# A hybrid decoder layer with product-key retrieval: the order ahead of the first slots, four weight products on GpSimd, and the last tile ended in pieces of three groups and one

## The reference, cut to what matters

```python
c_act = silu(c)
shift1, scale1, gate1, shift2, scale2, gate2 = split(c_act @ w_ada + b_ada)
h = modulate(rms_norm(x, g_norm1), shift1, scale1)
a, u, v = split(h @ w_in)                       # 1024 tokens, 512 columns each
mixed = concat(pool_mixer(a), spatial_gating(u, v))
x = x + gate1 * (mixed @ w_out)
h = modulate(rms_norm(x, g_norm2), shift2, scale2)
# product-key retrieval, for each token and each of 8 heads:
q = h @ w_query                                 # two halves ("sides") a head
s = q_side @ sub_keys_side                      # 128 scores a side
cand = top16(s_0) + top16(s_1)                  # 256 sums, the best 16 give idx
gate = softmax(best16)
act = gelu(expert_down[idx] . h)                # 16 rows of 1024
x = x + gate2 * sum(gate * act * expert_up[idx])
out = rms_norm(x, g_final)
```

## Time and profile before

| | |
|---|---|
| median of 3 runs | 2828.95 us (2825.89 to 2829.47) |
| the profiled execution | 2833.91 us, span 2832.1 us |
| busy in the span | PE 68%, DVE 67%, ACT 43%, POOL 40% |
| DMA | 1162.38 MB, mean 410 GB/s |
| HBM read, written | 1151.97 MB, 7.86 MB |

### The profile page before, as it was taken

One profiled execution on the slowest core, in us unless ns is written; L12 is line 12 of the kernel. 1 busy time (PEld: TensorE's weight loads), 2 busy tenths in 40 slices (PEclk: granted clock), 3 DMA queues, 4 the chain that ended last, 5 costly groups with the idle time before them and its releaser, 6 DMA issues.

```text
span 2832.1 us, 38640 instructions
## 1 busy us (share of the span) xinstructions
PE 1938.6 (68%) x13316; PEld 893.8 (32%) x13316; DVE 1894.8 (67%) x4714; ACT 1210.7 (43%) x3867; POOL 1123.1 (40%) x1030
## 2 busy tenths in 40 slices
PE   5898898888886566666656666665666666665553
PEld 4555354444442222232323222221322323221110
DVE  5686776785766567677666757677676756676454
ACT  1245445454453344454444434444343544344333
POOL 0044334344443254444444444444444444344342
PEclk9998898899886566665666667665766666576555
DMA  9899999999999999999999999999999999999997
GB/s 404 339 373 403 396 413 417 409 420 420 420 401 397 416 422 421 421 421 421 421 421 421 421 421 419 416 421 421 417 415 421 419 421 416 421 415 421 421 420 294
DMA packets 169221, 1162.38 MB, mean 410 GB/s; under 512 B 19009, under 2 KB 25665, under 8 KB 35778
## 3 DMA queue, kind: packets, MB, share of 16 engines
q0 software_dynamic: 147456, 1073.81, 91.9%
q1 hardware_dynamic: 21570, 86.11, 7.7%
HBM read 1151.97 MB, written 7.86 MB: 410 GB/s over the span
## 4 chain that ended last, share of the span: by engine, by line
DMA 54%; PE 22%; DVE 11%; ACT 6%; issue 3%; SPq 3%; POOL 0%; another core or an unknown queue 0%; DVEq 0%; POOLq 0%; ACTq 0%
DMA work<-experts,expert_rows 41%; DMA more_ring<-experts,expert_rows 8%; PE ps_sum L900 7%; DVE work L1560 5%; PE ps_small L866 5%; PE ps_m L815 4%; DMA work<-w_ada 2%; PE ps_m L759 2%; DMA weights<-experts,expert_rows 1%; ACT diag L1137 1%; ACT weight L1132 1%; DMA vn_u<-x_scratch 1%; PE ps_wide L841 1%; SPq L613 1%; PE ps_m L770 1%
## 5 line engine op out<-in xcount | busy, mean ns | idle before, releaser
L650 POOL DMA_INDIRECT work<-experts,expert_rows x818 | 899.0, 1099 | 1378.7 <-PE ps_sum L900 1225.8
L1560 DVE CUSTOM_DVE_ANT_0 work<-work 128x1024 f32<-128x1024 f32 x818 | 997.5, 1221 | 589.3 <-DMA work<-experts,expert_rows 573.4
L900 PE MATMUL ps_sum<-work,diag 128*32 128x256 f32 x6544 | 717.5, 523 | 674.7 <-ACT diag L1137 653.6
L1130 ACT ACTIVATE act_out<-act_in 128x1 f32<-128x1 f32 x1024 | 207.4, 203 | 1162.8 <-DVE act_in L1560 1141.9
L900 PEld LDWEIGHTS ps_sum<-work,diag 128*32 128x32 f32 x6544 | 150.1, 126 | 1146.5 <-ACT diag L1137 1052.1
L1137 ACT ACTIVATE diag<-const,weight 128x32 f32<-128x32 f32 x1024 | 329.2, 321 | 33.5
L1132 ACT ACTIVATE weight<-gate,act_out 128x1 f32<-128x1 f32 x1024 | 301.6, 295 | 33.3
L866 PE MATMUL ps_small<-h_t,weights 128*128 128x128 f32 x1344 | 291.2, 384 | 0.0
L866 PEld LDWEIGHTS ps_small<-h_t,weights 128*128 128x128 f32 x1344 | 249.3, 278 | 125.7 <-issue 120.4
L1560 DVE CUSTOM_DVE_ANT_0 more_ring<-more_ring,work 128x1024 f32<-128x1024 f32 x122 | 149.1, 1222 | 91.5 <-DMA more_ring<-experts,expert_rows 90.4
L650 POOL DMA_INDIRECT more_ring<-experts,expert_rows x122 | 134.8, 1105 | 180.3 <-PE ps_sum L900 175.5
(11 more groups left out here) (200 smaller groups left out, 1991.1 us busy)
## 6 DMA issues: line engine op xcount, KB each, us to landing
work<-w_ada SPq DMA_DIRECT2D x12, 2048.0 KB, 23.6
work<-sides SPq DMA_DIRECT2D x26, 576.0 KB, 8.4
work<-experts,expert_rows POOLq DMA_INDIRECT x818
weights<-sides SPq DMA_DIRECT2D x16, 576.0 KB
more_sides<-sides SPq DMA_DIRECT2D x12, 576.0 KB
weights<-w_in SPq DMA_DIRECT2D x3, 2048.0 KB, 17.2
x_buf<-x SPq DMA_DIRECT2D x8, 512.0 KB, 11.4
weights<-w_out SPq DMA_DIRECT2D x2, 2048.0 KB, 37.5
```

What stands on the lines that cost most here:

```text
L650: nc.gpsimd.indirect_dma_start(ring[x.ring], None, experts, bass.IndirectOffsetOnAxis(ap=rows_flat[:, x.column:x.column + 1], axis=0),).th ...
L900: last = nc.tensor.matmul(ps_sum[quarter(c), x.group, :], diag[:, x.ring, :], ring[x.ring][:, D + c * QCOLS:D + (c + 1) * QCOLS], start=x. ...
L1130: nc.scalar.activation(act_out[:, s:s + 1], act_in[:, s:s + 1], ACT.Gelu).then_inc(s_gelu, 1)
L1560: nc.vector.tensor_tensor_reduce(down, down, h2_spread[x.segment % 2], 1.0, 0.0, ALU.mult, ALU.add, act_in[:, x.g % TURN:x.g % TURN + 1]). ...
```

## The change

It has these parts:

- **The prologue's order.** On PE, side (1, 0) goes between the two halves of the first spread, side (1, 1) ahead of the move of routing 1, and that move ahead of scores (1, 1). Side (1, 3) goes into the slots (`SIDE_AT[0]`), and three of tile 1's four PROJECT_V steps too (`MIX_HEAD` is 6 in place of 9). ScalarE follows this order; `exp_logits(1)` comes right behind the second half of the first spread. SP issues one side load fewer ahead of the loop.
- **Slot numbers.** The mixers of tiles 2, 3 and 4 begin two slots later, tile 1's three later. Turn 1's route steps begin at slot 5 in place of 2. By the rule above the move of routing 2 then lies at slot 29.
- **The products of w_out and gate1.** GpSimd makes the four of them, behind the output projection of tile 0 and ahead of its first gather. VectorE's four are gone.
- **The last tile.** Its first piece has groups 0 to 2 and starts at slot 1008, its last piece group 3, which sums in a bank of its own (`ps_last`). The last piece's four stores are issued two by SP and two by ScalarE.

```diff
-MIX_HEAD = PROJECT_A
-MIX_AT = {1: -MIX_HEAD, 2: 31, 3: 70, 4: 109, 5: 150, 6: 190, 7: 230}
-SCALE_W_SLOTS = (3, 6, 9, 12)
+MIX_HEAD = PROJECT_V + 1
+MIX_AT = {1: -MIX_HEAD, 2: 33, 3: 72, 4: 111, 5: 150, 6: 190, 7: 230}
+SCALE_W_PARTS = 4
...
-SPLIT_SLOT = SLOTS * TILES - PAIR * PAIR * GATHERS
+SPLIT_SLOT = SLOTS * TILES - PAIR * GATHERS
-ENDS = [(t, 0, QUADS) for t in range(TILES - 1)] + [(TILES - 1, 0, 2), (TILES - 1, 2, QUADS)]
+ENDS = [(t, 0, QUADS) for t in range(TILES - 1)] + [(TILES - 1, 0, QUADS - 1), (TILES - 1, QUADS - 1, QUADS)]
...
-ROUTE_AT = [None, 2, 28, 50, 74, 98]
+ROUTE_AT = [None, 5, 28, 50, 74, 98]
...
+LAST_GROUP = {x.g for x in TABLE if (x.tile, x.group) == (TILES - 1, QUADS - 1)}
+SIDE_AT[0] = (1, 3)
...
+        ps_last = ps_m3[:, 0:QCOLS]
...
+        def store_last(queue, quarters):
+            t, first, last = ENDS[TILES]
+            queue.wait_ge(s_final, TILES + 1)
+            for c in quarters:
+                queue.dma_start(out_v[t, c][:, first:last, :], y[quarter(c), first:last, :]).then_inc(s_out, 16)
...
             # SP
-            for n in range(2, 6 + SIDE_BUFS):
+            for n in range(2, 5 + SIDE_BUFS):
                 load_side(*FIRST_USE[n])
...
-            store_out(TILES)
+            store_last(sp, range(QUADS // 2))
...
             # GpSimd
+            pool.wait_ge(s_o, 1)
+            pool.wait_ge(s_mod, 2)
+            for n in range(SCALE_W_PARTS):
+                part = w_out_sb[:, 2 * n:2 * n + 2, :]
+                nc.gpsimd.tensor_tensor(part, part, gate1[:, :].unsqueeze(1).to_broadcast([P, 2, D]),
+                                        ALU.mult).then_inc(s_scaled_w, 1)
             pool.wait_ge(s_gate2_ps, 2)
...
             # PE
-            for half in range(2):
-                spread_first_h2(0, half)
+            spread_first_h2(0, 0)
+            side(1, 0)
+            spread_first_h2(0, 1)
             mixer(TURN_H, 1)
-            for b in range(2):
-                side(1, b)
-                scores(1, b)
+            scores(1, 0)
+            side(1, 1)
+            move_choices(1)
+            scores(1, 1)
             for n in range(TURN_H + 1, MIX_HEAD):
                 mixer(n, 1)
-                if n == PROJECT_V + 1:
-                    move_choices(1)
-            for b in range(2, 4):
-                side(1, b)
-                scores(1, b)
+            side(1, 2)
+            scores(1, 2)
...
             # ScalarE
-            for half in range(2):
-                copy_spread(0, half)
-            for n in range(SCALE_H + 1, MIX_HEAD):
-                mixer(n, 1)
-            for b in range(4):
-                if b == 2:
-                    exp_logits(1)
-                copy_query(1, b)
-                copy_score(1, b)
+            copy_spread(0, 0)
+            copy_query(1, 0)
+            copy_spread(0, 1)
+            exp_logits(1)
+            copy_score(1, 0)
+            mixer(COPY_H, 1)
+            copy_query(1, 1)
+            mixer(COPY_H + 1, 1)
+            copy_score(1, 1)
+            copy_query(1, 2)
+            copy_score(1, 2)
...
-            act.wait_ge(s_ssq3, QUADS * (TILES - 1) + 2)
+            act.wait_ge(s_ssq3, QUADS * TILES - 1)
...
+            store_last(act, range(QUADS // 2, QUADS))
...
             # VectorE
-                if x.g in SCALE_W_SLOTS:
-                    scale_w_out(SCALE_W_SLOTS.index(x.g))
```

More of the change, by code:

```diff
@@ L154, in slot_table @@
                     x = Slot(len(table), r, group, (group * PAIRS + q) * GATHERS + i, len(starts) - 1)
-                    x.first = n == 0 and group % 2 == 0 and m == 0
+                    x.first = n == 0 and m == 0 and (group % 2 == 0 or (t, group) == (TILES - 1, QUADS - 1))
                     x.last = n == len(BATCHES[t]) - 1 and m == len(of_group) - 1
@@ L538, in load_x1_next @@
                 else:
-                    sp.wait_ge(s_scaled_w, len(SCALE_W_SLOTS))
+                    sp.wait_ge(s_scaled_w, SCALE_W_PARTS)
                     sp.wait_ge(s_x1_gated, 1)
@@ L809, in mixer @@
                         if t == 1:
-                            pe.wait_ge(s_scaled_w, len(SCALE_W_SLOTS))
+                            pe.wait_ge(s_scaled_w, SCALE_W_PARTS)
                     if n == PROJECT_OUT + 4:
@@ L899, in add_expert @@
                 for c in range(QUADS):
-                    last = nc.tensor.matmul(ps_sum[quarter(c), x.group, :], diag[:, x.ring, :],
+                    sums_of = ps_last if x.g in LAST_GROUP else ps_sum[:, x.group, :]
+                    last = nc.tensor.matmul(sums_of[quarter(c), :], diag[:, x.ring, :],
                                             ring[x.ring][:, D + c * QCOLS:D + (c + 1) * QCOLS],
@@ L1263, in gating_bias @@
                 last.then_inc(s_bias, 1)
-            def scale_w_out(n):
-                dve.wait_ge(s_o, 1)
-                dve.wait_ge(s_mod, 2)
-                part = w_out_sb[:, 2 * n:2 * n + 2, :]
-                nc.vector.tensor_tensor(part, part, gate1[:, :].unsqueeze(1).to_broadcast([P, 2, D]),
-                                        ALU.mult).then_inc(s_scaled_w, 1)
             def gate2_rows():
@@ L1575, in scale_sums @@
                     dve.wait_ge(s_out, 64 * t)
-                nc.vector.tensor_tensor(y[:, first:end, :], ps_sum[:, first:end, :],
+                sums_of = ps_last.unsqueeze(1) if n == TILES else ps_sum[:, first:end, :]
+                nc.vector.tensor_tensor(y[:, first:end, :], sums_of,
                                         gate2[:, :].unsqueeze(1).to_broadcast([P, end - first, QCOLS]),
```

## The result

The changed kernel takes 2837.23 us (median of 7 runs, 2830.51 to 2838.98) beside 2828.95 for the kernel before (7 runs, 2825.89 to 2832.24): a ratio of 1.0033 [1.0024, 1.0043]. It is slower by a third of a per cent, and lies outside the range forecast. The ratio is worked out from the single runs of both and isn't quite that of the two medians (1.0029 here); where this text turns a ratio into us, it takes the ratio: 0.0033 is 9.3 us. The profiled execution of the changed kernel took 2838.98 us, with a span of 2837.2; before had 2833.91 and 2832.1.

A forecast was written before the change was run, and what follows sets the result against it. The DMA engines were taken as the bound, so only their idle time at start and end counts. Start -3.6, tail -2.1 and GpSimd products +2.7 gave -3.0 us: 2826.0 us, range 2820.5 to 2832.0.

The forecast's parts named there:

- I take d = 3.0, between VectorE's own length and two passes: 2.7 us lost: Ahead of the first gather: each GpSimd product lasts 3.0 us and holds VectorE up, making that gather 2.7 us late.
- priced at only 4.8 us: Ahead of the first gather: with products of the skill's 4497 ns, it is 4.8 us late and the sum -0.9.
- the layout: From 82.3 us: GpSimd products laid between waiting VectorE instructions; column product 2.0, 4.8 or 8.0 us late for d = 2.28, 3.0, 3.8.
- Start: 4.6 - 1.0 = 3.6 us won: Start of the kernel: 4.6 us won by the new order, less 1.0 for late choices, without GpSimd's products.
- The 4.6 us: DMA idle time of 124 to 160 us: 2.5 us won ahead of gather 4 and 2.1 from 132 to 160.
- The 2.5 of them ahead of gather 4: From 124 to 132 us: gather 4 leaves 4.2 us earlier, so 2.5 of 3.4 us of idle DMA time are won.
- rival 4: Ahead of slot 0: the reordering does nothing, the gap only moves; +1.6, 2830.6 us; chance 0.06 with the rest.
- rival 3: At slots 32 to 63: late routing stops gathering, costing 8.8 us in place of 1.0; +4.8, 2833.7 us; chance 0.13.
- I take 1.0: Ahead of gather 32: late choices cost between nothing and near 9 us; 1.0 taken, as DMA engines set the pace.
- 2.1 were forecast: Last tile: stretch after the last dot 2.4 us shorter, less 0.3 us more DMA work ahead of the last rows.
- The bound of 0: Tail: nothing won if ScalarE's first store costs what two issues save and the earlier piece delays a slot.
- Rival 2: GpSimd's products, two passes each, hold VectorE up fully: +5.9 in place of 2.7; +0.2, 2829.2 us; chance 0.16.

The follow-up runs named there:

- e1: Changed kernel with the four products back on VectorE at slots 3, 6, 9 and 12: 2828.76 us, 1.0006 of the kernel before.
- e2: Changed kernel with turn 1's route steps from slot 4 in place of 5, so routing 2's choices move at slot 23: 2839.17 us, 1.0034.
- e3: Changed kernel with both the products back on VectorE and turn 1's route steps from slot 4: 2829.67 us, 1.0006 of the kernel before.
- e5: Kernel before with only the four products moved to GpSimd: 2841.09 us, 1.0036 of the kernel before.
- e7: Changed kernel with GpSimd's products cut into 16 of 128x512 in place of 4 of 128x2048: 2830.77 us, 0.9996 of the kernel before.
- e4: Kernel before with only the new end of the last tile: 2825.02 us, 0.9992 of the kernel before.
- e8: Kernel before with the new tail and only the reordering that brings exp_logits(1) forward, no work moved into slots: 2824.94 us, 0.9977 of the kernel before.
- groups 2 and 3: Sets of runs each timed on one chip, on the products and early exponential, then on single moved pieces; kernel before 2830.96 and 2830.11 us there.
- e12: Kernel before with new tail, early exponential and turn 1's route steps at slot 5 in place of 2, so routing 2's choices move at slot 29: 0.9978.
- r4: Kernel before with only the new end of the last tile, timed again in group 5 on one chip: 2825.10 us, 0.9993 of the kernel before.
- r8: Kernel before with the new tail and early exponential, timed again on one chip in group 5: 0.9992 of the kernel before.
- e13: Kernel before with new tail, early exponential, three V steps in slots, and mixers of tiles 2 to 4 three slots later: 2826.48 us, 0.9996.
- e9: Kernel before with new tail, early exponential and three of tile 1's PROJECT_V steps moved into slots 0 to 2: 1.0004 of the kernel before.

## Why the prediction was wrong

**GpSimd's products: mechanism right, size wrong.** The step "I take d = 3.0, between VectorE's own length and two passes: 2.7 us lost" failed. A product is 4.5 us long and the first gather 10.9 us late; the runs put the cost at 7.6 us (changed kernel against e1, timed apart) and 7.9 (e2 against e3, one chip) to 10.2 (e5 against before). Where the chosen row was far off is plain: one pass of GpSimd's memset was taken for half of a product of twice the elements, and it writes only. The Trainium skill's GPSIMD Engine Reference (section 3.1) gives 4497 ns for an addition of this size; the trace agrees for this product, with 4486 to 4527 for three of the four. But that length too was priced at only 4.8 us, for two reasons. First, the layout lets the column product in between the third product and the fourth, and it stops there: the diagonals, which the prediction names among those that would wait, would come right behind it, beside the fourth. (Laid out again for 4.5 us by the same rule, the column product is 6.4 us late and the first gather 4.3, not 4.8.) In the trace the column product began at 97.40, with the fourth product begun at 96.9, and had to wait for its end, 3.87 us for eight columns; the diagonals were then free. Second, the part of TensorE's work that ran at the lower level, behind waits of 3.59 and 5.05 us: 3.4 us of the chain, a term that no step had. Without the 0.9 us that the slower transposes took, the column product would have come at 96.5, ahead of the fourth product, but then the diagonals would have met it. That is argued, no run separates it.

**That exclusion is the cause of this cost is shown.** In the changed kernel only instructions whose two operands lie in SBUF are long, the one with an operand in PSUM is not, each is held just to the end of a product, and e7, with the same work in pieces of 1.27 us, takes the cost away. The cast held in e7 says that the kind isn't strictly two operands. In its SBUF — State Buffer page ("Who interferes with whom") the Trainium skill says that the engine which comes second is blocked fully until the first one's instruction ends. The rows agree in this direction too: 2.80 us for a statistic of 0.22, ended with the product.

**The order ahead of slot 0: right to slot 7, wrong behind it.** Gathers 4 and 7 came sooner than forecast, and the gaps of 124 to 160 all but went. What failed is "Start: 4.6 - 1.0 = 3.6 us won". Measured, the new order with its slot numbers lost 4.0 us (e1 against e4). Two terms fell.

The 4.6 us are not earned. The 2.5 of them ahead of gather 4 were read from one execution in which TensorE ran at a granted clock of 0.66 from 112 to 124; in two other executions of the old order 1.6 and 0.4 us stood idle from 112 to 132 in place of 4.4. And e8, which only brings gather 4 forward, has as much idle DMA time from 112 to 160 us as e4 (4.5 and 4.1). It gained 0.6 us over the tail on one chip (0.9992 against 0.9993; the intervals allow 2 to 3 us), so at that place rival 4 was right, at least nearly. In groups 2 and 3 e8 and e12 stood at 0.9977 and 0.9978, with medians of 2824.7 to 2824.9, where e4, r4 and r8 had 2824.5 to 2825.1 on theirs; what moved was before. That difference between chips stays open.

And the moved work has a price that the prediction had at nothing, since it let the DMA engines set the pace in the slots: three V steps 5.4 to 7.4 us, where they take 5.4 us on TensorE, and a side with its score 4.5 us, where they take 2.5. These prices don't add up: e1 has both, and the later mixers too, and is only 4.0 us over the tail and 4 to 8 over e8. So the runs show that moving this work costs, and not that each us comes back as one. That TensorE comes to lag behind among the slots 30 to 95, where e1 loses its lead, is what the shares and the table suggest. Whether it is by its load alone, or since the mixer of tile 1 now ends closer to that of tile 2, isn't settled: e13, which opens that gap, is lower than e9 by 0.0008, on another chip.

**The late choices: rival 3 fell as a cause.** GpSimd did wait, for 8.8 to 12 us, where the rival set a stop of 8.8. But e3, without that wait, has the time of e1, which has it, on the same chip; e12 and e8, and e2 and the changed kernel, agree too, timed apart. The rows in the queue covered it. The step "I take 1.0" was sound; the price measured is 0, give or take an interval of 0.0009. That the wait stands beside a share of 0.77 in the changed kernel misleads: taken away, the gap moved on to 232 to 344.

**The tail: right.** The stretch is shorter by 2.4 us and the ratio by 0.0007 to 0.0008, 2.0 to 2.3 us; 2.1 were forecast. The bound of 0 didn't come true: ScalarE's two issues (0.87) run beside SP's two (0.79).

**The sum.** Tail -0.0008, order +0.0014, products +0.0027: +0.0033. That this is the ratio measured proves nothing, since each term is the difference of two kernels in a row from before to the changed one; it says where the time went. Of the miss of 12 us (forecast -3.0, measured 9.3), 7.6 are the order's and 4.9 the products'; the tail took 0.2 back. Rival 2 had the side of the products right and their size too small; no rival had the order cost anything but by the late choices.

**The better versions.** The changed kernel is beaten by e4, e8 and e12, by 0.0040 to 0.0056, all timed apart from it. They beat the kernel before by 0.0007 to 0.0023, with an interval clear of 1 only for e8 and e12 in groups 2 and 3.

## What to carry to other kernels

An engine without work isn't free when its instructions and another engine's hold each other up, as GpSimd's and VectorE's do here: price each by its whole length on the partner's smallest instruction in the chain, and cut it into pieces no longer than the partner can wait. Before closing a gap, see in a second execution whether it is there at all. A gap that is closed is won only if the same us are not asked for again at a place where nothing covers them: work moved from the prologue into slots in which TensorE is busy for nine tenths of the time cost here, for each of two moves alone, at least what it took on TensorE. When a wait stands beside a gap, take the wait away alone and see whether the gap goes or only moves.

## What the hardware showed

- A VectorE instruction of one column (0.22 us) took 2.80 us beside a GpSimd product, one of eight columns (0.17 us) 4.04. Each side waits until the other's instruction ends, GpSimd's gather too; the trace writes the wait into the duration. An instruction with one operand in PSUM kept its 1.29 us.
- The product of 128x2048 takes GpSimd 4.5 us and VectorE 2.28; one of 128x512 takes GpSimd 1.27, so 16 of them are 20.3 us of work, where four long ones are 18.1; with the waits 22.8 and 18.9.
- After a TensorE wait of 5.05 us, 32 matmuls took 6.37 in place of 3.81 us. The granted clock from 84 to 104 us was 0.75 in place of 1.00.
- Three executions of the same order ahead of slot 0 issued gather 4 at 129.4, 125.1 and 122.5 us, with a granted clock of 0.66, 0.95 and 1.00 from 112 to 124.
- The kernel before had medians from 2826.86 to 2830.96 us on the chips of the five groups, with 21 to 33 runs each: 0.15% between chips, as much as most of the effects sought here.
